# Gate product in single-pass operands, and a new VectorE order of states, sums and low parts around the plane copies

## Chip, cores and metric

The kernel runs on one core of one Trainium2 chip. The metric is the device time of one execution in microseconds (us). Before the change three runs gave 1149.07, 1149.14 and 1149.42 us; the median is 1149.14 us.

## What is computed

A two-layer encoder trunk over 512 tokens of width 1024. Layer 0 mixes tokens with two groups of gated linear attention heads, layer 1 with multi-head latent attention; each is followed by a squared-ReLU MLP. The change lies in layer 0's mixer, which in the reference is, per head:

```python
S_t = diag(exp(log_g_t)) S_{t-1} + k_t v_t^T ;  o_t = S_t^T q_t
# group A (HGRN2): forget = lb + (1-lb)*sigmoid(hf); k = 1-forget; log_g = log(forget)
# group B (GLA):   log_g = log_sigmoid(ga @ w_gate + b_gate) / 16
o = rmsnorm(o, norm) * silu(gate)
mix = concat([o_a, o_b]) @ w_out
```

`ga` has 16 columns and comes out of the input projection; `ga @ w_gate` is the gate product. The outputs are held to float32-like accuracy, so most products are made of three: an operand is split into a high part (an fp32r tile) and a low part (what is left), and high x low, low x high and high x high are summed (`mm3`, lines 1938 to 1940).

## The kernel before

The mixer's eight heads lie in six packs: two of GLA with two heads each, four of HGRN2 with one. The eight heads are numbered `o` = 0 to 7 in the order of the packs. A hand-written table, `SLOTS`, sets the order of the work on every engine: 46 slots, in each of which TensorE projects one tile (a key, query, value, gate or forget tile; 24 products of 128x512 for the projected ones) or turns a value tile or makes a gate product (`z`, slots 2 and 9). With each slot go, at fixed places, `items` (the decayed keys and queries of the pack ahead), `groups` (a step of the planes of the pack behind), `end` (the pack whose cumulative sums close the slot), and the lists OUTPUTS, SQUARES, SUMS and MIXES of heads.

The words of the trace's lines: a plane is one level of the masked key-query products of a head, made on TensorE in `pairs` (L2094, L2107) and copied through a mask by VectorE in `group` (L1539). A pack has seven planes, in the steps (0, 1), (2, 3), (4, 5), (6). After step 2 TensorE makes the chunk states (`chunk_states`, L2156) and VectorE chains them (`update_state`, L1513 and L1515). `outputs` (L2119, then L2123) waits for a head's plane 6 and, before L2123, for the pack's states. ScalarE squares the head's output (`head_square` L1039, `head_copy` L1045 and L1048), VectorE takes the square's low part (`square_low`, L1495), TensorE sums it (`head_sum`, L2134), ScalarE makes the inverse root (L898, L899), VectorE multiplies (`head_gate`, L1500 and L1503), ScalarE takes the high part (`head_high`, L1058) and VectorE the low part (`head_low`, L1507). `cumulate` (L1490) makes a pack's cumulative sums, from which GpSimd makes the differences `dec` (L831). `clamp` (L1457, L1462) reads a forget or gate tile out of its PSUM bank; ScalarE makes the sigmoid (L996 to L998); the gate's product with it is L1476. `split_high` (L636) and `split_low` (L645) split a weight unit.

Each engine runs its own list in order. Waits that matter here:

- One buffer, `sq[:, 1, :]`, holds the head being mixed. `head_copy` of head `o` (L1048) overwrites it and so waits until `head_low` of head `o - 1` has read it: `act.wait_ge(mix_ready, o)`. `head_sum(o)` waits for that copy: `pe.wait_ge(o_read, o + 1)`.
- Two PSUM banks take the projected tiles in turn. A bank is free when its tile two before has been read; for a gate tile that is when L1476 has run. Gate tile 7 is the last one (slot 37); after it TensorE fills the output projection's banks, token block 0 in the bank of gate 6, block 1 in the bank of gate 7.
- `pairs` of the last pack waits for the plane copies before it; `transpose_keys` waits for the states of the pack before.

In slot 21 (tile `q` of pack 3) VectorE's list is: `head_gate(0)`, three items, `cumulate(3)`, `head_low(0)`, `square_low(1)`, the step-2 `group` of heads 2 and 3 with the state, then slot 22. In slots 36 and 37 it is: items, `head_low(5)`, step-2 `group` of head 6 with the state, `clamp` of gate 7, the step-3 `group` of head 6.

Of the kernel before, what the change touches and what calls it, by code (L numbers as in the profile page):

```python
# [5 lines left out]
ALU = mybir.AluOpType  # L6
ACT = mybir.ActivationFunctionType
F32 = mybir.dt.float32
F32R = mybir.dt.float32r
# [3 lines left out]
P = 128  # L13
T = 512
# [7 lines left out]
HEADS = 4  # L22
GLA_DK = 64
GATE_RANK = 16
# [4 lines left out]
STEPS = [(0, 1), (2, 3), (4, 5), (6,)]  # L29
# [27 lines left out]
def trunk(nc, x, positions, norm_gains, ev_w_in, hg_lb_table, gla_w_gate, gla_b_gate, hg_out_norm,  # L57
# [39 lines left out]
    for st in range(8):  # L97
# [11 lines left out]
        n = len(long_)  # L109
# [3 lines left out]
        for a in range(1, n):  # L113
            i = long_[a]
# [43 lines left out]
    tile_no = {}  # L158
# [152 lines left out]
    with ExitStack() as ctx:  # L311
        def sb(name, shape, dt=F32, scope=ctx):
            return scope.enter_context(nc.sbuf_tensor(name, shape, dt))
# [15 lines left out]
        gbc = sb("gbc", [P, D])  # L329
        vec = sb("vec", [P, V_ROWS])  # L330
        lbt = sb("lbt", [P, 6, HEADS])
        w_gate = sb("w_gate", [2 * GATE_RANK, HEADS * GLA_DK])
        ropec = sb("ropec", [P, 2])
        tmp = sb("tmp", [P, 2, T])
        tok = sb("tok", [P, 16, NT])
# [13 lines left out]
        with ExitStack() as s1:  # L349
            sb("under_s1", [P, KD, 2, T], F32, s1)  # L350
            x_tok = sb("x_tok", [P, NT, D], F32, s1)
            vrows = sb("vrows", [V_ROWS, P], F32, s1)
        with ExitStack() as s2:
            sb("under_s2", [P, KD, 2, T], F32, s2)
            xl = sb("xl", [P, LEVELS, T], F32, s2)
            dec = sb("dec", [P, 3, T], F32, s2)
            kq_sb = sb("kq_sb", [P, 2, 2, T], F32, s2)
            b_sb = sb("b_sb", [P, T], F32, s2)
            qe0 = sb("qe", [P, T], F32, s2)
            vbuf = sb("vbuf", [P, 4, T], F32, s2)  # L360
            ke = sb("ke", [P, T], F32, s2)
            e_last = sb("e_last", [P, 2, NT], F32, s2)
            a_sb = sb("a_sb", [P, 4, P], F32, s2)
            ke_t = sb("ke_t", [P, NT - 1, P], F32, s2)
            state = sb("state", [P, NT - 1, P], F32, s2)
            t_f = sb("t_f", [P, T], F32, s2)
            t_g = sb("t_g", [P, T], F32, s2)
            ga_t = sb("ga_t", [2 * GATE_RANK, T], F32, s2)
        with ExitStack() as s3:
            sb("under_s3", [P, KD, 2, T], F32, s3)  # L370
            v_tok = sb("v_tok", [P, NT, D], F32, s3)
# [269 lines left out]
        def split_low(dve, u, i=0):  # L641
            dve.wait_ge(hi_ready, u + 1 + BODY * i)
            for src, hi, lo, g in pieces(u):
                if g is None:
                    ins = nc.vector.tensor_tensor(lo, src, hi.bitcast(F32), ALU.subtract)  # L645
                else:
                    ins = nc.vector.scalar_tensor_tensor(out=lo, in0=src, scalar=vec[:, g:g + 1], in1=hi.bitcast(F32),  # L647
                                                         op0=ALU.mult, op1=ALU.subtract)
            ins.then_inc(lo_ready, 1)
# [20 lines left out]
        def halves(ap, L):  # L670
            return ap.rearrange("p (b h j) -> p b h j", h=2, j=L)

        def gain(layer, n, k):
            c = gain_col(layer, n, k)
            return vec[:, c:c + 1]
# [121 lines left out]
        def _(pool):  # L797
# [4 lines left out]
            nc.gpsimd.affine_select(out=ident[:, :], in_=ident[:, :], compare_op=ALU.not_equal, fill=1.0, base=0,  # L802
                                    pattern=[[-1, P]], channel_multiplier=1).then_inc(consts_ready, 1)
            ch.link(nc.gpsimd.memset(masks[:, :, :], 0.0))
            for r, c in ((slice(0, 64), slice(64, 128)), (slice(0, 32), slice(32, 64)), (slice(64, 96), slice(96, 128))):
                ch.link(nc.gpsimd.memset(masks[r, 0, c], 1.0))
            for lv in range(2, LEVELS):
# [86 lines left out]
        def _(act):  # L894
# [73 lines left out]

            n = tile_no[("ga", 0)]
            wait_tile(act, n)  # L970
            nc.scalar.copy(ga_t[:, :], bank[n % 2][0:2 * GATE_RANK, :]).then_inc(ga_ready, 1)
            pump(unit_no[("ga", 0)])

            def decay(p, lv):
# [401 lines left out]
        def _(dve):  # L1376
# [41 lines left out]
            ch.link(nc.vector.tensor_tensor(lbt[:, 1, :], t0, lbt[:, 0, :], ALU.subtract))  # L1418
            nc.vector.tensor_tensor(lbt[:, 2, :], t1, lbt[:, 0, :], ALU.subtract).then_inc(vec_ready, 1)
            split_low(dve, 3)  # L1420
            dve.wait_ge(vec_ready, 3)
            ch.link(nc.vector.tensor_tensor(lbt[:, 0, :], lbt[:, 1, :], lbt[:, 2, :], ALU.add))
            ch.link(nc.vector.reciprocal(lbt[:, 3, :], lbt[:, 0, :]))
            ch.link(nc.vector.tensor_tensor(lbt[:, 4, :], lbt[:, 1, :], lbt[:, 3, :], ALU.mult))
            ch.link(nc.vector.tensor_scalar(lbt[:, 5, :], lbt[:, 4, :], -1.0, 1.0, ALU.mult, ALU.add))
            dve.wait_ge(x_split[START], 2 * NT)
            nc.vector.memset(pp[0][:, :, :], 0.0).then_inc(p_zero, 1)
            dve.wait_ge(consts_ready, 4)
# [93 lines left out]
            def group(lead, step):  # L1522
                heads = heads_of(PACK_OF[lead])
                if step == 0:
                    for o in heads:
                        if o < 4:
                            nc.vector.memset(a_bufs[o], 0.0).then_inc(a_zero, 1)
                        else:
                            dve.wait_ge(o_done, o - 3)
                for plane in STEPS[step]:  # L1530
                    for o in heads:
                        n = plane_no(o, plane)
                        dve.wait_ge(p_done, n + 1)
                        if plane:
                            dve.wait_ge(a_ready, plane_no(o, plane - 1) + 1)
                        elif o < 4:
                            dve.wait_ge(a_zero, o + 1)
                        mask = masks[:, plane:plane + 1, :].to_broadcast([P, NT, P])
                        nc.vector.copy_predicated(a_bufs[o % 4], mask.bitcast(I32), plane_bank(n)).then_inc(a_ready, 1)  # L1539
                if step == 2:  # L1540
                    update_state(PACK_OF[lead])

            for i, (tile, col, items, groups, end) in enumerate(SLOTS):
                if tile is not None:
                    if tile[0] in "fg":
                        clamp(*tile)
                    if i == IDLE_SLOT - 1:
                        for o, c in groups:
                            group(o, c)
                    if col is not None:  # L1550
                        wait_tile(dve, tile_no[tile])
                        if len(groups) < 2:
                            split_low(dve, unit_no[tile] + SPLIT - 1)
                    evacuate(*tile)
                if i == IDLE_SLOT:
                    split_low(dve, EO + SPLIT - 1)
                for o in SQUARES[i - 1] if i >= 1 else ():
                    if o not in WHOLE_SUMS + SOON_SUMS:
                        square_low(o)
                for o in MIXES[i]:  # L1560
                    head_gate(o)
                planes_first = len(items) > 4
                if planes_first:
                    for o, c in groups:
                        group(o, c)
                for p, lv in items:
                    decayed(p, lv)
                if end is not None:
                    cumulate(end)
                for o in MIXES[i]:  # L1570
                    head_low(o)
                for o in SQUARES[i]:
                    if o in SOON_SUMS:
                        square_low(o)
                for o, c in groups if not planes_first and i != IDLE_SLOT - 1 else ():
                    group(o, c)
                if col is not None and len(groups) > 1:
                    split_low(dve, unit_no[tile] + SPLIT - 1)
                if i in EXT_SLOTS:
                    split_low(dve, EXT_SLOTS[i])  # L1580
# [355 lines left out]
        def _(pe):  # L1936
# [111 lines left out]
            def project(tile, col):  # L2048
                n = tile_no[tile]
                what, i = tile  # L2050
                if what == "z":
                    pe.wait_ge(ga_ready, 1)
                    wait_bank(pe, n)
                    nc.tensor.matmul(bank[n % 2][:, :], w_gate[:, i * P:(i + 1) * P], ga_t[:, :], start=True,
                                     stop=True).then_inc(tile_done, 1)
                    return
                if what == "w":
                    pe.wait_ge(v_raw, i + 1)
                    if tile not in APART:
                        wait_bank(pe, n)  # L2060
                    elif i == 2:
                        pe.wait_ge(v_ready, 1)
                    for t in range(NT):
                        ins = nc.tensor.transpose(tile_bank(tile)[:, t * P:(t + 1) * P],
                                                  vbuf[:, i % 4, t * P:(t + 1) * P], ident[:, :])
                    ins.then_inc(tile_done, 1)
                    return
                feature_tile(unit_no[tile], n, h_hi, h_lo)
# [459 lines left out]
```

## Time and profile before

| | us |
|---|---|
| median of the three runs | 1149.14 |
| the profiled execution, its own time | 1148.82 |
| its span in the trace | 1147.10 |
| TensorE busy (98% of the span) | 1129.7 |
| VectorE busy (70%) | 802.0 |
| ScalarE busy (55%) | 626.9 |

All times below count from the span's start. The mixer of layer 0 takes about the first 250 us. A busy share of TensorE counts matmuls whose ends are modelled, so that the start-to-start step of matmuls (0.23 us for 128x512 in fp32r) says more than their durations (0.39 us). In a row of the timeline the bracket is the idle time of that engine ahead of the instruction, with what ended it.

### The profile page before, as it was taken

What the parts mean: (1) busy time and instruction counts of PE and PEld (TensorE: products, weight loads), DVE (VectorE), ACT (ScalarE), POOL (GpSimd) and SP (SyncE); (2) the same over time, 40 slices, a digit from 0 to 9 for tenths busy, and PEclk for the clock granted to TensorE, in tenths of its full rate; (3) what the DMA queues carried; (4) which work ended last, traced back from release to release, by engine and by line L of the source; (5) the groups of instructions that cost most, each with busy time, mean ns of one, the idle gap of its engine ahead of it and who ended that gap; (6) DMA issues with size and microseconds to landing.
All of it is one profiled execution on the core that took longest, in us unless ns stands there. A gap on an engine that the chain in (4) does not pass through costs nothing.

```text
span 1147.1 us, 18687 instructions
## 1 busy us (share of the span) xinstructions
PE 1129.7 (98%) x7053; PEld 941.4 (82%) x7053; DVE 802.0 (70%) x1197; ACT 626.9 (55%) x1168; POOL 130.4 (11%) x129
## 2 busy tenths in 40 slices
PE   9999999999999999999999999999999999999997
PEld 7787787778988888888888988888988888888886
DVE  6567888866578767767666578846578768768564
ACT  6654675646645554554447766646645545544432
POOL 2432333200222111110000001000000000000000
PEclk9999999999999999999999999999999999999999
DMA  5322222263233233231323323104342233231321
GB/s 173 102 81 57 76 56 57 75 202 110 90 123 110 92 110 128 74 127 37 110 81 82 107 56 91 47 27 139 110 147 93 88 114 110 91 111 42 105 74 74
DMA packets 87596, 108.36 MB, mean 94 GB/s; under 512 B 10290, under 2 KB 48291, under 8 KB 87524
## 3 DMA queue, kind: packets, MB, share of 16 engines
q1 hardware_dynamic: 85780, 101.87, 28.0%
q0 software_dynamic: 1744, 5.51, 1.6%
q8 instruction: 48, 0.79, 0.3%
q14 instruction: 24, 0.20, 0.1%
HBM read 104.22 MB, written 2.10 MB: 93 GB/s over the span
## 4 chain that ended last, share of the span: by engine, by line
PE 87%; DVE 6%; ACT 4%; issue 2%; DMA 0%; POOL 0%; DVEq 0%; ACTq 0%; SPq 0%
PE bank L1938 22%; PE bank L1940 22%; PE bank L1939 22%; PE pp L1938 3%; PE pp L1940 3%; PE pp L1939 3%; PE po L2466 2%; PE pp L2001 1%; PE po L1940 1%; PE po L1939 1%; PE po L1938 1%; PE pp L2447 1%; DVE tmp L1539 1%; ACT w_hi L638 1%; PE pp L2107 1%
## 5 line engine op out<-in xcount | busy, mean ns | idle before, releaser
L1938 PE MATMUL bank<-h_lo,w_hi 128*128 128x512 f32 (+1 forms) x724 | 277.2, 383 | 0.6 <-DVE y L1476 0.6
L1940 PE MATMUL bank<-h_hi,w_hi 128*128 128x512 f32 (+1 forms) x724 | 274.3, 379 | 0.0
L1939 PE MATMUL bank<-h_hi,w_lo 128*128 128x512 f32 (+1 forms) x724 | 274.3, 379 | 0.0
L1938 PEld LDWEIGHTS bank<-h_lo,w_hi 128*128 128x128 f32 x724 | 136.2, 188 | 28.4 <-issue 2.7
L1940 PEld LDWEIGHTS bank<-h_hi,w_hi 128*128 128x128 f32 x724 | 136.2, 188 | 25.7
L1939 PEld LDWEIGHTS bank<-h_hi,w_lo 128*128 128x128 f32 x724 | 136.2, 188 | 24.5
L636 ACT CAST wx<-raw 128x1024 fp32r<-128x1024 f32 x72 | 74.6, 1049 | 97.3 <-DVE raw L1631 66.0
L1938 PE MATMUL bank<-wx,a_hl 128*128 128x512 f32 x320 | 125.3, 392 | 0.0
L1940 PE MATMUL bank<-wx,a_hl 128*128 128x512 f32 x320 | 124.6, 389 | 0.0
L1939 PE MATMUL bank<-wx,a_hl 128*128 128x512 f32 x320 | 124.5, 389 | 0.0
L1642 DVE TENSOR_TENSOR y<-y,bank 128x512 f32<-128x512 f32 x80 | 54.8, 685 | 86.8 <-PE bank L1940 86.6
L645 DVE TENSOR_TENSOR wx<-raw,wx 128x1024 fp32r<-128x1024 f32 x72 | 87.9, 1221 | 28.2 <-ACT wx L636 27.9
L647 DVE SCALAR_TENSOR_TENSOR w_lo<-stage,vec,w_hi 128x512 fp32r<-128x512 f32 (+3 forms) x124 | 76.9, 672 | 9.8 <-ACT w_hi L638 9.8
L831 POOL TENSOR_TENSOR dec<-b_sb 128x512 f32<-128x512 f32 x48 | 67.2, 1422 | 142.6 <-DVE b_sb L1490 59.8
L638 ACT ACTIVATE w_hi<-stage,vec 128x512 fp32r<-128x512 f32 (+3 forms) x124 | 74.6, 656 | 14.9 <-DMA stage<-in_mlp_w 14.3
L645 DVE TENSOR_TENSOR w_lo<-stage,w_hi 128x1024 fp32r<-128x1024 f32 x44 | 57.5, 1308 | 21.0 <-ACT w_hi L636 11.7
L1940 PEld LDWEIGHTS bank<-wx,a_hl 128*128 128x128 f32 x320 | 60.1, 188 | 12.5
L1939 PEld LDWEIGHTS bank<-wx,a_hl 128*128 128x128 f32 x320 | 60.1, 188 | 12.2
L1938 PEld LDWEIGHTS bank<-wx,a_hl 128*128 128x128 f32 x320 | 60.1, 188 | 12.3
L636 ACT CAST w_hi<-stage 128x1024 fp32r<-128x1024 f32 (+1 forms) x45 | 46.1, 1026 | 14.5 <-DMA stage<-in_mlp_w 8.9
L1136 ACT ACTIVATE tmp<-bank 128x512 f32<-128x512 f32 x26 | 15.6, 598 | 59.9 <-PE bank L1940 59.7
L1938 PE MATMUL bank<-w_lo,a_hl 128*128 128x512 f32 x112 | 45.2, 404 | 0.0
(406 smaller groups left out, 2175.3 us busy)
## 6 DMA issues: line engine op xcount, KB each, us to landing
stage<-in_mlp_w SPq DMA_DIRECT2D x66, 512.0 KB, 3.8
raw<-in_mlp_w SPq DMA_DIRECT2D x50, 512.0 KB, 3.5
stage<-in_ev_w_in SPq DMA_DIRECT2D x28, 512.0 KB, 3.8
spare<-in_mlp_w SPq DMA_DIRECT2D x12, 512.0 KB, 4.6
stage<-in_ev_w_out SPq DMA_DIRECT2D x8, 512.0 KB, 3.5
stage<-in_od_w_out SPq DMA_DIRECT2D x8, 512.0 KB, 3.5
x_tok<-in_x SPq DMA_DIRECT2D x4, 512.0 KB, 4.9
xr<-in_x POOLq DMA_DIRECT2D x4, 512.0 KB, 4.3
```

The costliest lines, as they stand in the source:

```text
L636: ins = nc.scalar.copy(hi, src)
L638: ins = nc.scalar.activation(hi, src, ACT.Copy, scale=vec[:, g:g + 1])
L645: ins = nc.vector.tensor_tensor(lo, src, hi.bitcast(F32), ALU.subtract)
L647: ins = nc.vector.scalar_tensor_tensor(out=lo, in0=src, scalar=vec[:, g:g + 1], in1=hi.bitcast(F32), op0=ALU.mult, op1=ALU.subtract)
L831: nc.gpsimd.tensor_tensor(dec[:, item % 3, :].rearrange("p (b j) -> p b j", j=2 * L), b_sb[:, :].rearrange("p (b j) -> p b j", j=2 * L), r ...
L1136: nc.scalar.activation(f, src[:, :], ACT.Relu).then_inc(up_read, 1)
L1539: nc.vector.copy_predicated(a_bufs[o % 4], mask.bitcast(I32), plane_bank(n)).then_inc(a_ready, 1)
L1642: nc.vector.tensor_tensor(dst, dst, banks[src][:, :], ALU.add).then_inc(prod_read, 1)
L1938: nc.tensor.matmul(dst, wh, xl_, start=first, stop=False)
L1939: nc.tensor.matmul(dst, wl, xh, start=False, stop=False)
L1940: return nc.tensor.matmul(dst, wh, xh, start=False, stop=last)
L2466: ins = nc.tensor.matmul(po[:, kb * P:T], v_tok[:, kb, h * P:(h + 1) * P], turned_probs(h)[:, kb, kb * P:T], start=(kb == 0), stop=(kb == ...
```

## The change

1. The gate product. `ga_t` and the gate weights become fp32r tiles of 128 rows: rows 0 to 31 hold the high part, 32 to 63 the low part of `ga` against the high part of the weights, 64 to 95 the high part of `ga` against the low part of the weights, 96 to 127 zeros. One product over 128 rows gives the sum of all three.
2. `update_state` runs after the last step of a pack (plane 6) in place of after step 2.
3. In a slot with cumulative sums, and in slot 36, `cumulate` and `head_low` come behind the slot's plane copies. Of the slots with `head_low` that is slots 21 and 36. `cumulate` changes its place in slots 16, 21 and 27.
4. In slot 37 the `clamp` of gate 7 comes behind the slot's `group` (now with the state).

```diff
-        w_gate = sb("w_gate", [2 * GATE_RANK, HEADS * GLA_DK])
+        gate_w = sb("gate_w", [P, HEADS * GLA_DK], F32R)
...
-            ga_t = sb("ga_t", [2 * GATE_RANK, T], F32, s2)
+            ga_t = sb("ga_t", [P, T], F32R, s2)
...
+            ch.link(nc.gpsimd.memset(ga_t[6 * GATE_RANK:P, :].bitcast(F32), 0.0))
+            ch.link(nc.gpsimd.memset(gate_w[6 * GATE_RANK:P, :].bitcast(F32), 0.0))
...
-            nc.scalar.copy(ga_t[:, :], bank[n % 2][0:2 * GATE_RANK, :]).then_inc(ga_ready, 1)
+            nc.scalar.copy(ga_t[GATE_HIGH, :], bank[n % 2][0:2 * GATE_RANK, :]).then_inc(vec_ready, 1)
+            act.wait_ge(vec_ready, 4)
+            nc.scalar.copy(ga_t[GATE_HIGH_AGAIN, :], ga_t[GATE_HIGH, :].bitcast(F32)).then_inc(vec_ready, 1)
+            act.wait_ge(vec_in, 16 * 10)
+            for r in (GATE_HIGH, GATE_LOW):
+                nc.scalar.copy(gate_w[r, :], w_gate[:, :]).then_inc(vec_ready, 1)
...
+            dve.wait_ge(vec_ready, 4)
+            nc.vector.tensor_tensor(ga_t[GATE_LOW, :], bank[tile_no[("ga", 0)] % 2][0:2 * GATE_RANK, :],
+                                    ga_t[GATE_HIGH, :].bitcast(F32), ALU.subtract).then_inc(ga_ready, 1)
             dve.wait_ge(vec_ready, 3)
...
+            dve.wait_ge(vec_ready, 7)
+            nc.vector.tensor_tensor(gate_w[GATE_HIGH_AGAIN, :], w_gate[:, :], gate_w[GATE_HIGH, :].bitcast(F32),
+                                    ALU.subtract).then_inc(ga_ready, 1)
...
-                if step == 2:
+                if step == len(STEPS) - 1:
                     update_state(PACK_OF[lead])
...
-                    if tile[0] in "fg":
-                        clamp(*tile)
                     if i == IDLE_SLOT - 1:
                         for o, c in groups:
                             group(o, c)
+                    if tile[0] in "fg":
+                        clamp(*tile)
...
-                if end is not None:
-                    cumulate(end)
-                for o in MIXES[i]:
+                lows_first = i != IDLE_SLOT - 2 and end is None
+                for o in MIXES[i] if lows_first else ():
                     head_low(o)
                 for o in SQUARES[i]:
                     if o in SOON_SUMS:
                         square_low(o)
                 for o, c in groups if not planes_first and i != IDLE_SLOT - 1 else ():
                     group(o, c)
+                if end is not None:
+                    cumulate(end)
+                for o in MIXES[i] if not lows_first else ():
+                    head_low(o)
...
-                    pe.wait_ge(ga_ready, 1)
+                    pe.wait_ge(ga_ready, 2)
+                    pe.wait_ge(consts_ready, 4)
...
-                    nc.tensor.matmul(bank[n % 2][:, :], w_gate[:, i * P:(i + 1) * P], ga_t[:, :], start=True,
+                    nc.tensor.matmul(bank[n % 2][:, :], gate_w[:, i * P:(i + 1) * P], ga_t[:, :], start=True,
```

`SOON_SUMS` holds head 1 alone; its `square_low` is in slot 21. `IDLE_SLOT` is 38.

## Rows read from the trace of the kernel before

**Rows 1.** The page, part 1: busy time, share of the span, instructions of each engine.

```profile
PE 1129.7 (98%) x7053; PEld 941.4 (82%) x7053; DVE 802.0 (70%) x1197; ACT 626.9 (55%) x1168; POOL 130.4 (11%) x129
```

**Rows 2.** Waits of PE over the whole run: total us, times, longest.

```profile
PE po L2119 <- DVE tmp L1539: 3.9, 2, 2.4
```

**Rows 3.** Timeline, PE, the first gate product: start, us, engine, line, operation, tiles.

```profile
28.71 0.39 PE L1940 MATMUL bank<-h_hi,w_hi 128*128 128x512 f32 x1
29.03 1.12 PE L2054 MATMUL bank<-ga_t,w_gate 32*128 32x512 f32 x2
30.08 0.50 PE L1938 MATMUL bank<-h_lo,w_hi 128*128 128x512 f32 x1
```

**Rows 4.** Timelines of DVE, ACT and PE around the start of slot 0.

```profile
22.58 0.15 DVE L1422 TENSOR_TENSOR lbt<-lbt 128x4 f32<-128x4 f32 x1
...
25.77 1.23 DVE L645 TENSOR_TENSOR w_lo<-stage,w_hi 128x1024 fp32r<-128x1024 f32 x1 [1.21 <-ACT w_hi L636]
...
24.59 1.05 ACT L636 CAST w_hi<-stage 128x1024 fp32r<-128x1024 f32 x1 [2.35 <-DMA stage<-in_ev_w_in]
...
23.47 0.40 PE L1938 MATMUL bank<-h_lo,w_hi 128*128 128x512 f32 x1
```

**Rows 5.** Timeline, DVE, from the cumulative sums of slot 21 to the state.

```profile
127.00 1.36 DVE L1490 TENSOR_TENSOR_SCAN b_sb<-ones,t_f 128x128 f32<-128x128 f32 x4
128.28 0.67 DVE L1507 TENSOR_TENSOR a_hl<-sq,a_hl 128x512 fp32r<-128x512 f32 x1
128.86 0.69 DVE L1495 TENSOR_TENSOR sq_lo<-sq,sq_hi 128x512 fp32r<-128x512 f32 x1
129.46 0.74 DVE L1539 COPY_PREDICATED tmp<-gbc,pp 128x512 f32<-128x512 int32 x1
...
131.93 0.29 DVE L1513 COPY state<-misc 128x128 f32<-128x128 f32 x1
```

**Rows 6.** Timeline, ACT and PE, slots 21 and 22: copy and sum of head 1.

```profile
128.98 0.60 ACT L1048 ACTIVATE sq<-po 128x512 f32<-128x512 f32 x1 [2.70 <-DVE a_hl L1507]
...
129.77 0.42 PE L2134 MATMUL po<-sq_lo,ones 128*128 128x512 f32 x1
...
130.86 0.76 PE L2107 MATMUL pp<-kq_sb 64*32 64x32 f32 x64 [0.43 <-DVE rinv L1539]
```

**Rows 7.** Timeline, PE, slot 33: outputs of head 5 and the products behind.

```profile
199.65 1.13 PE L2119 MATMUL po<-tmp,vbuf 128*128 128x128 f32 x8 [1.54 <-DVE tmp L1539]
...
201.71 1.01 PE L2094 MATMUL pp<-xl 128*64 128x64 f32 x21
```

**Rows 8.** Timeline, DVE, slots 36 to 38.

```profile
226.28 0.68 DVE L1507 TENSOR_TENSOR a_hl<-sq,a_hl 128x512 fp32r<-128x512 f32 x1
226.88 1.58 DVE L1539 COPY_PREDICATED tmp<-gbc,pp 128x512 f32<-128x512 int32 x2
228.34 0.29 DVE L1513 COPY state<-misc 128x128 f32<-128x128 f32 x1
228.67 0.73 DVE L1515 SCALAR_TENSOR_TENSOR state<-state,e_last,misc 128x128 f32<-128x128 f32 x2
...
229.92 0.72 DVE L1539 COPY_PREDICATED tmp<-gbc,pp 128x512 f32<-128x512 int32 x1
...
232.09 0.69 DVE L1476 TENSOR_TENSOR y<-bank,t_g 128x512 f32<-128x512 f32 x1 [0.34 <-ACT t_g L998]
...
235.66 0.66 DVE L1495 TENSOR_TENSOR sq_lo<-sq,sq_hi 128x512 fp32r<-128x512 f32 x1
```

**Rows 9.** Timeline, PE, outputs of head 6, the fill of block 1, the sum.

```profile
230.79 1.95 PE L2119 MATMUL po<-tmp,vbuf 128*128 128x128 f32 x8 [2.40 <-DVE tmp L1539]
...
234.31 0.48 PE L1938 MATMUL bank<-w_lo,a_hl 128*128 128x512 f32 x1
...
237.93 0.50 PE L2134 MATMUL po<-sq_lo,ones 128*128 128x512 f32 x1
```

**Rows 10.** Windows: PE, PEld, DVE, ACT, POOL busy, PEclk, DMA share, GB/s.

```profile
232.00:233.00 1.00, 1.00 (x7) 1.00 (x7) 0.69 (x1) 0.99 (x2) 0.00 (x0) 0.50 0.29 25
```

More of the change, by code:

```diff
@@ L352, in trunk @@
             vrows = sb("vrows", [V_ROWS, P], F32, s1)
+            w_gate = sb("w_gate", [2 * GATE_RANK, HEADS * GLA_DK], F32, s1)
         with ExitStack() as s2:
@@ L671, in halves @@
             return ap.rearrange("p (b h j) -> p b h j", h=2, j=L)
+        GATE_HIGH, GATE_LOW, GATE_HIGH_AGAIN = [slice(r, r + 2 * GATE_RANK) for r in (0, 2 * GATE_RANK, 4 * GATE_RANK)]
         def gain(layer, n, k):
```

## The prediction, made before any run of the change

> **What bounds the kernel.** I read the page's busy shares first: TensorE is busy for 1129.7 of the span's 1147.10 us [rows 1], so time is won either by giving it less work or by closing its gaps. The list of its waits says where the gaps are that another engine makes: the largest entry is 3.9 us in two waits of `outputs` for a plane copy [rows 2]. The timelines put them at slot 33 (1.54 us, head 5) [rows 7] and behind slot 37 (2.40 us, head 6) [rows 9]. The second costs more than its 2.40 us: the granted clock, 1.0 before, reads 0.50 behind it (1.2 in place of 2.4 GHz) [rows 10]. From the outputs to the next product TensorE takes 234.31 - 230.79 = 3.52 us there [rows 9], and 201.71 - 199.65 = 2.06 us for the same work at slot 33 [rows 7], where the clock held. My price of one fall of the clock is the difference, about 1.5 us. Elsewhere TensorE runs without a gap and hands its delay on, so what slot 22 loses reaches the end.
>
> **Part 1, the gate product.** Two products stand on TensorE's path. For one, the start before it to the start behind it is 30.08 - 28.71 = 1.37 us [rows 3]. A 128x512 product in fp32r has a step of 0.23 us, so the same stretch would be 0.46 us and each product gives back 0.91 us: **-1.82 us** for two (the other, in slot 9, shows the same stretch). What bounds it: nothing, if the new product should run as the old one, and 2 x 0.91. I take the upper end, since an fp32r product over 128 rows is the kernel's commonest row [rows 3]. The row shows two records of the old product, in 1.12 us [rows 3]. The Trainium skill, "FP8 and Floating Point Precision", TensorE Precision Notes, says that a true FP32 product takes four passes through the array; by that rule three of four steps go, an estimate of 3 x 0.23 = 0.69 us for each product and a term of -1.38 us. The trace's stretch is longer than four steps, and the row decides.
>
> The operands cost work at the start, where I find cover for all. ScalarE adds one small copy and two casts; it stands idle 2.35 us for a load just there [rows 4], and three pieces of 32 rows cost no more than the 0.5 to 0.6 us that 512 columns cost it elsewhere [rows 6]. VectorE adds two low parts, 0.7 us each at most (0.69 us for 128x512 out of PSUM [rows 8]), ahead of an idle time of 1.21 us [rows 4]. The first of them now frees the bank that the `q` tile of slot 1 writes from 23.47 on [rows 4]: starting near 22.6, where L1422 stands now [rows 4], it ends near 23.3 and TensorE sees it near 23.4. The margin is 0.1 us; if it fails, it costs up to 0.5 us. GpSimd adds two memsets ahead of the masks' last flag, which nobody needs before about 24 us; no queue of loads is touched.
>
> **Part 2, slot 21.** This is the part that I think costs. Before, VectorE runs the sums at 127.00, `head_low(0)` at 128.28, `square_low(1)` at 128.86, four plane copies from 129.46 to 131.93 [rows 5]. After: `square_low` at 127.00, copies from 127.60 to 130.07 (2.47 us), sums to 131.35 (1.28 us), and `head_low(0)` only then, 131.35 in place of 128.28: 3.07 us later. ScalarE is standing in its list at the copy of head 1, L1048, for just that instruction: it waited 2.70 us and began 0.70 us behind the start of `head_low` [rows 6]. So the copy begins at 132.05, ends at 132.65, and `head_sum(1)` can start at 132.75. Before, it started at 129.77 with no idle ahead of it [rows 6]: TensorE now waits 2.98 us. The earlier copies spare it the 0.43 us that it waited for a plane at 130.86 [rows 6], and from 132.75 to the next planes is 0.55 us: they start at 133.30 in place of 130.86, **+2.44 us**. Queued behind the waiting copy on ScalarE are the value tile of slot 22, the inverse root and a weight's cast, all late by 3 us but none needed at once. On TensorE everything is queued behind it.
>
> Its idle time, less the modelled end of the last matmul, is about 2.8 us. One of 1.54 us left the clock alone, one of 2.40 us brought it down; 2.8 is nearest to the second, so I add one fall, **+1.5 us**, with 0 as the other end.
>
> In slots 16 and 27 `cumulate` moves too. There VectorE waits for TensorE's next tile afterwards, and GpSimd's differences are needed only in the items two slots on: nothing.
>
> **Part 3, states last.** In slot 33 the wait for head 5's plane ends earlier by the state's time, 228.34 to about 229.32 = 0.98 us by the same row elsewhere [rows 8]. I book no gain: from there to slot 37 VectorE's chain does not wait for TensorE, so TensorE arrives early and waits again. In the other packs no plane copy is waited for.
>
> **Part 4, slots 36 and 37.** Plane 6 of head 6 moves from 229.92 to 228.34 (copies from 226.28, then the low part of 0.60 us) [rows 8], 1.58 us earlier, and so `outputs(6)`, to 229.21, with a gap of 1.5 us ahead. But the clamp of gate 7 now stands behind that plane and the state and begins near 229.93 in place of 229.32. ScalarE's sigmoid and the product L1476 follow: 232.70 in place of 232.09 [rows 8]. That product frees the bank of block 1's fill. TensorE, through with outputs and transposes at about 231.3 at full clock, waits there about 2.15 us, to 233.48, against 234.31 before [rows 9]. The fill is 12 products of 0.23 us; `head_sum(6)` then meets the low part of its square, 0.61 us late, 236.27 in place of 235.66 [rows 8], done near 237.04. Before it ran at 237.93 [rows 9]: **-0.9 us**. The bounds are -1.58 us (the whole plane's gain) and +0.61 us (VectorE's delay passed on). A fall of the clock here would cost 1.5 us of this; 2.15 us lies between the two gaps known, in two pieces with 2 us of work between, so I take none.
>
> **Sum.** -1.82 + 2.44 + 1.5 - 0.9 = +1.2 us. On the profiled execution's own 1148.82 us (span 1147.10 and 1.72 around it) that is 1150.0; the median of the runs stands 0.32 us higher, so **1150.4 us**. What this measurement can tell from no change is about 0.2%, 2.3 us.
>
> **The rivals.**
> - *No fall of the clock* at slot 22: -1.82 + 2.44 - 0.9 = -0.3, 1148.9 us. For it: 2.8 us is beyond any gap seen here, so the fall is an inference from one row; against it, a shorter gap fell.
> - *Two falls*, the other side: the wait for gate 7's bank, which the later clamp makes, brings the clock down a second time. Place: ahead of block 1's fill; price: another 1.5 us, 1151.9 us in all, slower by 0.24%. It decides once 2.15 us is idle enough. For it: 2.15 is nearer to 2.40 than to 1.54. Against it: the 2 us of matmuls just before.
> - *No stall in slot 22*: if ScalarE's copy of head 1 comes in time after all, the term and its fall go, with 0.43 us: -1.82 - 0.43 - 0.9 = -3.15, 1146.0 us. Against it: ScalarE's 2.70 us wait for exactly this low part [rows 6], and a sum that started on time by 0.2 us only.
> - *The gate product is not shorter*, if it should still be made in passes: the first term goes, 1152.2 us. Against it: every split product's row.
>
> **How the numbers follow.** One fall (at either place; they cost the same) 0.40, none 0.20, two 0.22, no stall 0.10, no shorter product 0.03, something unseen 0.05, shared out. The likeliest is one fall, 1150.4 us. The range takes in none and two falls, 1148.9 to 1151.9, wider by up to 1 us below (the tail's better bound) and 0.6 us above (the start's margin): 1147.9 to 1152.5. Faster by over 0.2% (below 1146.8) needs the stall not to come: 0.12 with the unseen. Slower by over 0.2% (above 1151.4) is most of two falls, the longer product and the rest: 0.23. Within 0.2%: 0.65.
>
> **What would show it.** Part 1: L2054 with one record and a step of 0.23 us, twice, and slot 1's `q` tile starting without idle. Part 2: L2134 in slot 22 with about 3 us idle ahead of it, released by ScalarE's L1048, that by L1507 behind the scans, and PEclk 0.50 for some us behind. Part 3: no 1.54 us ahead of head 5's outputs, but the same time of head 6's to VectorE. Part 4: outputs of head 6 about 1.6 us earlier against VectorE, and a new wait of about 2 us ahead of block 1's fill, released by L1476. The prediction is wrong if `head_sum(1)` starts on time, if the clock stays at 1.0 throughout or falls twice, or if a gap behind 250 us swallows or adds some of it.

## The result, and the profile after

Seven runs of the changed kernel gave a median of **1152.86 us** (1152.26 to 1153.85), against 1149.32 for seven runs of the kernel before beside them. The ratio of the two is 1.0037, with a 95% interval from 1.0027 to 1.0046: slower by 3.5 us, or 0.3%. A later session gave 1152.56 against 1149.21, ratio 1.0031 [1.0020, 1.0042]. The forecast was 1150.4, and its range ended at 1152.5. The profiled execution took 1152.5 us. Of the fifteen runs of the two sessions the five slowest (1153.05 us and above) have a mean granted clock of 0.996 over the whole span, the ten others 0.997 or 0.998, as has the profiled one.

The page of the changed kernel, its span and part 1:

```profile
span 1150.8 us, 18690 instructions
...
PE 1129.0 (98%) x7051; PEld 941.4 (82%) x7051; DVE 802.7 (70%) x1199; ACT 628.6 (55%) x1171; POOL 133.5 (12%) x131
```

TensorE lost two of its records (the old gate products were two each) and is busy for about as long as before [rows 1]. The span grew by 3.7 us all the same, so the time went into gaps. The waits of PE, total us, times and longest, show which:

```profile
PE bank L1957 <- DVE y L1492: 3.6, 2, 2.1
PE po L2154 <- ACT sq L1058: 2.8, 1, 2.8
...
PE po L2139 <- DVE tmp L1555: 1.7, 2, 0.9
PE bank L1957 <- ACT kq_sb L1022: 1.1, 2, 0.6
```

The 3.9 us of `outputs` [rows 2] fell to 1.7. In their place stand 2.8 us of a head's sum (slot 22), a wait of 2.1 us at the fill for gate 7's product (its other entry, 1.5 us, is at slot 33), and, in the last row, two waits for `kq_sb` that the prediction does not contain. Their place is behind the two gate products. The timeline, PE and ACT:

```profile
29.52 0.40 PE L1959 MATMUL bank<-h_hi,w_hi 128*128 128x512 f32 x1
29.76 0.39 PE L2074 MATMUL bank<-ga_t,gate_w 128*128 128x512 f32 x1
30.70 0.47 PE L1957 MATMUL bank<-h_lo,w_hi 128*128 128x512 f32 x1 [0.55 <-ACT kq_sb L1022]
...
29.96 0.60 ACT L1022 ACTIVATE kq_sb<-bank 128x512 f32<-128x512 f32 x1 [1.76 <-PE bank L1959]
...
54.44 0.47 PE L1957 MATMUL bank<-h_lo,w_hi 128*128 128x512 f32 x1 [0.55 <-ACT kq_sb L1022]
```

The new product is one record of 0.39 us, as forecast. But the value tile behind it goes into the bank of the `q` tile two before it, and ScalarE can read that tile out (0.60 us) only after its last product of 29.52. From that product to the value tile is 1.18 us, against 1.37 before [rows 3]: 0.19 us won in place of 0.91. Of the whole old stretch, only this much stood beyond ScalarE's read.

Slots 21 and 22, timelines of DVE, ACT and PE:

```profile
127.41 0.69 DVE L1511 TENSOR_TENSOR sq_lo<-sq,sq_hi 128x512 fp32r<-128x512 f32 x1
128.01 0.74 DVE L1555 COPY_PREDICATED tmp<-gbc,pp 128x512 f32<-128x512 int32 x1
...
130.47 1.36 DVE L1506 TENSOR_TENSOR_SCAN b_sb<-ones,t_f 128x128 f32<-128x128 f32 x4
131.74 0.67 DVE L1523 TENSOR_TENSOR a_hl<-sq,a_hl 128x512 fp32r<-128x512 f32 x1
...
132.45 0.60 ACT L1058 ACTIVATE sq<-po 128x512 f32<-128x512 f32 x1 [5.75 <-DVE a_hl L1523]
...
133.19 0.47 PE L2154 MATMUL po<-sq_lo,ones 128*128 128x512 f32 x1 [2.84 <-ACT sq L1058]
...
133.92 0.90 PE L2127 MATMUL pp<-kq_sb 64*32 64x32 f32 x64
```

The low part stands behind the copies and the sums, 131.74 in place of 128.28 [rows 5]; the copy of head 1 follows 0.71 us behind its start, and the sum waits 2.84 us. The windows behind it (PEclk is the third column from the end) show what the gap brings:

```profile
133.00:134.00 1.00, 0.81 (x11) 0.38 (x19) 0.55 (x1) 0.53 (x2) 1.00 (x1) 0.82 0.00 0
134.00:135.00 1.00, 1.00 (x65) 0.94 (x66) 0.11 (x1) 0.94 (x2) 1.00 (x2) 0.50 0.23 55
...
136.00:137.00 1.00, 1.00 (x3) 0.75 (x3) 0.93 (x4) 0.32 (x1) 0.51 (x1) 0.50 0.90 269
137.00:138.00 1.00, 1.00 (x6) 0.78 (x5) 0.20 (x1) 0.00 (x0) 0.00 (x0) 0.97 0.03 8
```

The clock granted to TensorE is 1.2 GHz for a little over 3 us. Slots 33 and 37, timelines of PE and DVE:

```profile
203.18 1.13 PE L2139 MATMUL po<-tmp,vbuf 128*128 128x128 f32 x8 [0.80 <-DVE tmp L1555]
...
208.63 0.47 PE L1957 MATMUL bank<-h_lo,w_hi 128*128 128x512 f32 x1 [1.48 <-DVE y L1492]
...
233.68 1.13 PE L2139 MATMUL po<-tmp,vbuf 128*128 128x128 f32 x8 [0.89 <-DVE tmp L1555]
237.90 0.50 PE L1957 MATMUL bank<-w_lo,a_hl 128*128 128x512 f32 x1 [2.09 <-DVE y L1492]
...
241.54 0.50 PE L2154 MATMUL po<-sq_lo,ones 128*128 128x512 f32 x1
...
232.81 0.72 DVE L1555 COPY_PREDICATED tmp<-gbc,pp 128x512 f32<-128x512 int32 x1
...
234.39 0.68 DVE L1478 TENSOR_SCALAR t_g<-bank 128x512 f32<-128x512 f32 x1
...
237.15 0.69 DVE L1492 TENSOR_TENSOR y<-bank,t_g 128x512 f32<-128x512 f32 x1 [0.95 <-ACT t_g L1008]
```

At slot 33 the wait for the plane fell from 1.54 [rows 7] to 0.80, and TensorE waited longer at the next gate tile instead, 1.48 us against 0.61 before. At slot 37 the outputs waited 0.89 us in place of 2.40 [rows 9], and a new wait of 2.09 us stands ahead of the fill. In this execution the clock held there.

The lateness of the changed kernel against the trace of before, at six places, gives the balance (us; each term is the change of the lateness):

| from the row before to the row after | lateness | term | forecast |
|---|---|---|---|
| last product ahead of the first gate product, 28.71 to 29.52 | 0.81 | start +0.81 | 0 |
| value tile behind the second, 54.03 to 54.44 | 0.41 | gate products -0.40 | -1.82 |
| planes of slot 22, 130.86 to 133.92 | 3.06 | slot 22 +2.65 | +2.44 |
| clamp of the forget tile behind them, 137.32 to 141.59 | 4.27 | its half clock +1.21 | +1.5 |
| sum of head 6, 237.93 to 241.54 | 3.61 | tail -0.66 | -0.9 |
| span, 1147.1 to 1150.8 | 3.70 | rest +0.09 | 0 |

The rows of the half clock's term, DVE, before and after:

```profile
137.32 0.69 DVE L1457 TENSOR_SCALAR t_f<-bank 128x512 f32<-128x512 f32 x1 [1.93 <-PE bank L1940]
141.59 0.69 DVE L1473 TENSOR_SCALAR t_f<-bank 128x512 f32<-128x512 f32 x1 [4.39 <-PE bank L1959]
```

### The profile page after: what moved, and what is told of

It is laid out like the page before. It is cut to its first block, busy times and chain, and to the rows that moved or that the text cites. A ratio compares the mean times of both kernels' runs of the same rounds, so it can differ in the third digit from the quotient of the medians.

```text
span 1150.8 us, 18690 instructions
## 1 busy us (share of the span) xinstructions
PE 1129.0 (98%) x7051; PEld 941.4 (82%) x7051; DVE 802.7 (70%) x1199; ACT 628.6 (55%) x1171; POOL 133.5 (12%) x131
## 4 chain that ended last, share of the span: by engine, by line
PE 80%; DVE 4%; ACT 3%; issue 1%; DMA 0%; POOL 0%; DVEq 0%; ACTq 0%; SPq 0%
PE bank L1957 21%; PE bank L1959 20%; PE bank L1958 20%; PE pp L1957 3%; PE pp L1958 3%; PE pp L1959 3%; PE po L2486 2%; PE pp L2020 1%; PE po L1959 1%; PE po L1957 1%; PE po L1958 1%; PE pp L2467 1%; ACT w_hi L639 1%; DVE tmp L1555 1%; PE pp L2271 1%
## 5 line engine op out<-in xcount | busy, mean ns | idle before, releaser
L836 POOL TENSOR_TENSOR dec<-b_sb 128x512 f32<-128x512 f32 x48 | 69.6, 1471 | 143.8 <-DVE b_sb L1506 66.6
L646 DVE TENSOR_TENSOR w_lo<-stage,w_hi 128x1024 fp32r<-128x1024 f32 x44 | 56.7, 1289 | 19.9 <-ACT w_hi L637 10.8
```

What stands on the lines that cost most here:

```text
L836: nc.gpsimd.tensor_tensor(dec[:, item % 3, :].rearrange("p (b j) -> p b j", j=2 * L), b_sb[:, :].rearrange("p (b j) -> p b j", j=2 * L), r ...
```

## The experiments

Each ran beside the kernel before in its own session: that kernel's median was 1148.91 us for the first four, 1148.78 for the next four and 1149.21 for the last.

**Low part early (e1).** The change with one condition less, so that in slot 21 `head_low(0)` stands ahead of the copies again and the sums stay behind them:

```diff
-                lows_first = i != IDLE_SLOT - 2 and end is None
+                lows_first = i != IDLE_SLOT - 2
```

> The changed kernel, with one condition taken back: head_low stays ahead of the plane copies in the slots with cumulative sums (in effect slot 21). Theory A (the loss is head 1's sum in slot 22, which waits for ScalarE's copy, that for head_low(0) behind the sums, 2.8 us of idle time and about 1.4 us of a lowered clock): the wait ahead of head_sum(1) goes, the clock stays at 1.0 there, the 0.43 us wait for a plane goes too, and the time is 3.9 to 4.3 us below the changed kernel, about 1148.7. Rival B (the loss is the sums themselves, made later, so that GpSimd's differences come late): the sums still stand behind the planes, the time stays near 1152.9.

Measured: 1147.76 us, ratio 0.9996 [0.9987, 1.0005]. By the ratios that is 4.7 us less than the change, somewhat more than expected. The timeline, PE:

```profile
129.98 0.39 PE L2154 MATMUL po<-sq_lo,ones 128*128 128x512 f32 x1
...
130.53 0.76 PE L2127 MATMUL pp<-kq_sb 64*32 64x32 f32 x64
...
233.13 0.50 PE L1957 MATMUL bank<-w_lo,a_hl 128*128 128x512 f32 x1 [2.09 <-DVE y L1492]
```

Neither the sum nor the planes behind it wait. The place of one instruction in VectorE's list is the whole loss of slot 22.

**The gate product alone (e2).** The kernel before with part 1 of the change and VectorE's old order.

> The kernel before with the gate product's part of the change alone. As predicted before the result, it would be 1.8 us faster (1147.5). Theory A now: each shorter product only uncovers TensorE's wait for the bank that the q tile filled, until ScalarE has read it (about 0.55 us idle behind each product), so that 0.2 us each are left: -0.4 us, 1148.9. Rival C (the operands' work at the start delays the first projected tiles by the 0.7 us that the profile of the changed kernel shows): +0.3 us, 1149.6, with the q tile of slot 1 starting after an idle time that ends with VectorE's low part.

Measured: 1148.55 us, ratio 0.9994 [0.9985, 1.0003]: no change that can be told, and not the 1.82 us. Its trace has the two waits of 0.55 us for `kq_sb`, the first of them in this row of PE:

```profile
30.97 0.47 PE L1954 MATMUL bank<-h_lo,w_hi 128*128 128x512 f32 x1 [0.55 <-ACT kq_sb L1022]
```

**Sums and low part behind the planes alone (e3).** The kernel before with part 3 of the change in the slots with sums.

> The kernel before with one part alone: in the slots with cumulative sums, sums and head_low stand behind the plane copies. Theory A: this alone costs what the change costs in slot 22, 2.4 us of moved start and about 1.4 us of clock: +3.9 us, 1153.2, with the wait of 2.8 us ahead of head_sum(1) and PEclk 0.50 behind it. If the loss needs another part of the change as well: between 1149.3 and 1151.

Measured: 1153.45 us, ratio 1.0035 [1.0021, 1.0048]: alone, this part costs as much as the whole change. Its wait is longer than the 2.84 us, since the state still stands in slot 21 ahead of the sums. The timeline, PE:

```profile
134.10 0.77 PE L2137 MATMUL po<-sq_lo,ones 128*128 128x512 f32 x1 [3.63 <-ACT sq L1048]
```

**The tail alone (e4).** The kernel before with the states last and the new order in slots 36 and 37.

> The kernel before with the states last and the new order of slots 36 and 37 (low part behind the planes, clamp of gate 7 behind both groups). Theory A: outputs of head 6 come 1.6 us earlier, the fill of token block 1 waits some 2 us for gate 7's bank, the clock does not fall: -0.6 to -0.9 us, 1148.6. Rival D (a second fall of the clock at that wait): +0.7 us, 1150.

Measured: 1149.72 us, ratio 1.0005 [0.9996, 1.0014]. Timeline, PE:

```profile
229.30 1.13 PE L2122 MATMUL po<-tmp,vbuf 128*128 128x128 f32 x8 [0.76 <-DVE tmp L1539]
233.51 0.50 PE L1941 MATMUL bank<-w_lo,a_hl 128*128 128x512 f32 x1 [2.09 <-DVE y L1476]
```

Both waits are those of the changed kernel, but here the granted clock fell behind the second: 0.66, 0.50, 0.50 and 0.63 in the four us from 234 on.

**States last alone (e5).**

```diff
-                if step == 2:
+                if step == len(STEPS) - 1:
```

> The kernel before with the states updated last in each slot, and nothing else. In slot 37 the copy of plane 6 of head 6 no longer stands behind the state: it should begin at about 228.95 in place of 229.92, so head 6's outputs should start near 229.8 in place of 230.79, with about 1.4 us idle ahead. The clamp of gate 7 keeps its place, so its product with the sums, L1476, should stay at 232.09 and the fill of block 1 be released near 232.5 with a new wait of about 1 us. Theory A (the tail is a race of two chains, plane 6 and gate 7's product, and its price is the later of them plus a fall of the clock if a gap is long): both gaps are below 1.54 us, which left the clock alone, head 6's sum starts near 236.0 in place of 237.93, and the time is about 2 us below before. Rival B (what the tail gains is taken up by a later wait, as in slot 33): the same rows but a time within 0.5 us of before. Rival C (states last helps nothing, as the prediction booked for the other packs): head 6's outputs near 230.8 as before.

Measured: 1147.52 us, ratio 0.9989 [0.9980, 0.9998]. Timeline, PE:

```profile
230.44 1.13 PE L2119 MATMUL po<-tmp,vbuf 128*128 128x128 f32 x8 [1.56 <-DVE tmp L1539]
233.02 0.50 PE L1938 MATMUL bank<-w_lo,a_hl 128*128 128x512 f32 x1 [0.46 <-DVE y L1476]
```

This one line is worth 1.3 us, because plane 6 of head 6 then stands ahead of the state while gate 7's clamp keeps its early place. Both waits are short and the clock holds: theory A, with a smaller sum (about 2 us were expected). Against e4, the later clamp and low part of slots 36 and 37 give back 1.8 us (0.9989 to 1.0005), a fall of the clock included.

**A bank of their own for the gate products (e6, e9).** The test of the failed step: e6 is e2, and e9 the changed kernel, with the gate products in a PSUM bank outside the turn of the two. The tiles between the two gate products change banks with each other, so that the turn of the rest stays unbroken (not shown here):

```diff
-        APART = {("w", 0): po[:, :], ("w", 1): flat[3], ("w", 2): po[:, :]}
+        APART = {("w", 0): po[:, :], ("w", 1): flat[3], ("w", 2): po[:, :], ("z", 0): misc[:, :], ("z", 1): misc[:, :]}
...
-                    wait_bank(pe, n)
-                    nc.tensor.matmul(bank[n % 2][:, :], gate_w[:, i * P:(i + 1) * P], ga_t[:, :], start=True,
+                    if i >= 1:
+                        pe.wait_ge(z_read, i)
+                    nc.tensor.matmul(tile_bank(tile), gate_w[:, i * P:(i + 1) * P], ga_t[:, :], start=True,
```

> The kernel before with the new gate product alone, as in e2_gate_only, but the two gate products are written to a bank of their own, outside the turn of the two banks that the other tiles share. Theory A (the product is short, and what ate its gain is the wait of the next value tile for ScalarE's reading of the q tile, two tiles back in the same bank): the two waits of 0.55 us for kq_sb go, the stretch from the product before a gate product to the product behind it falls from 1.18 us in the changed kernel to about 0.5, and the time is about 1.3 us below e2_gate_only and 1.7 below before. Rival B (the value tile would wait for something else that ends at the same time, such as a transposed block or a weight): the waits stay at 0.5 us under another name and the time is that of e2_gate_only. Rival C (TensorE runs ahead by the 1.3 us and gives it back at the next wait of VectorE, at slots 33 and 37): the waits go but the time moves by less than 0.5 us.

Measured for e6: 1147.23 us, ratio 0.9980 [0.9971, 0.9989]. The timeline, PE, the product before, the gate product and the value tile, and then head 6's outputs:

```profile
29.69 0.40 PE L1960 MATMUL bank<-h_hi,w_hi 128*128 128x512 f32 x1
29.92 0.39 PE L2076 MATMUL misc<-ga_t,gate_w 128*128 128x512 f32 x1
30.16 0.39 PE L1958 MATMUL bank<-h_lo,w_hi 128*128 128x512 f32 x1
...
229.74 1.27 PE L2141 MATMUL po<-tmp,vbuf 128*128 128x128 f32 x8 [2.44 <-DVE tmp L1559]
```

The stretch is 0.47 us and the waits are gone: 0.90 us won for each product, the prediction's 0.91. By the ratios e6 is 1.6 us below e2, where 1.3 were expected.

> The changed kernel with its two gate products in a bank of their own, and nothing else different: the term that the prediction booked at 1.82 us and that came out near 0.4. The stretches around the gate products should fall from 1.18 us to 0.47 us as in e6_gate_own_bank. If what is won there reaches the end: about 1.4 us below the changed kernel of the same session. If slot 22's wait for VectorE takes it up (TensorE arrives 1.4 us earlier at the first heads' sum, and VectorE's chain does not follow TensorE there): the wait of 2.84 us grows by up to 1.4 us and the time is within 0.5 us of the changed kernel.

Measured for e9: 1151.10 us beside 1152.56 of the changed kernel in the same session, 1.46 us less (1150.09 to 1152.44 and 1151.61 to 1153.49); expected were 1.4. Its wait in slot 22 stayed at 2.84 us, so nothing was taken up there.

**Low part early and own bank (e7).** e1 and e9 together.

> The changed kernel with the sums behind the planes but the head's low part ahead of them in every slot (e1_low_early), and the gate products in a bank of their own. If the two terms add: e1_low_early showed 1147.8 us, so about 1.3 us less, 1146.5, without a wait at the first heads' sum and without the 0.55 us waits. If the gain of the gate products is taken up at VectorE's waits in slots 33 and 37 (TensorE arrives earlier and waits longer): the time is that of e1_low_early, and the waits ahead of outputs at slots 33 and 37 are longer by what was gained, which may also bring a fall of the clock at the second, +1.5 us.

Measured: 1146.81 us, ratio 0.9981 [0.9972, 0.9990], the first case. Some of the gain is lost where the clock falls behind the 2.09 us wait ahead of the fill, as it did in the profiled execution.

**Low part ahead of the sums (e10).** The changed kernel with these two exchanged:

```diff
-                if end is not None:
-                    cumulate(end)
                 for o in MIXES[i] if not lows_first else ():
                     head_low(o)
+                if end is not None:
+                    cumulate(end)
```

> The changed kernel with the head's low part still behind the plane copies in slot 21, but ahead of the sums, not behind them. The copy on ScalarE that waits for it should come 1.28 us earlier, and the wait of TensorE ahead of the first heads' sum be 2.84 - 1.28 = about 1.56 us, which is the length of the wait at slot 33 that left the clock alone. If the clock's fall hangs on the wait's length: no half clock behind it, and the time is 1.28 + 1.5 = 2.8 us below the changed kernel, near 1150.0. If any wait at this place brings the clock down: only 1.3 us below, near 1151.5.

Measured: 1151.16 us, 1.40 below the changed kernel's 1152.56. The number is that of the second case; the trace is not. Timeline and windows, PE:

```profile
131.92 0.47 PE L2154 MATMUL po<-sq_lo,ones 128*128 128x512 f32 x1 [1.58 <-ACT sq L1058]
```

```profile
133.00:134.00 1.00, 1.00 (x34) 0.87 (x26) 1.00 (x2) 0.97 (x3) 1.00 (x1) 1.00 0.00 0
236.00:237.00 1.00, 1.00 (x5) 0.77 (x4) 1.00 (x2) 1.00 (x4) 0.00 (x0) 0.64 0.34 129
237.00:238.00 1.00, 1.00 (x4) 0.81 (x3) 0.90 (x3) 1.00 (x2) 0.00 (x0) 0.50 0.30 59
```

The wait shrank to 1.58 us as worked out and the clock held behind it, but it fell at the tail, behind the same 2.09 us that had left it alone in the changed kernel. In this execution the fall was moved, not saved.

**Second looks (e11, e12).** The changed kernel and the kernel before, unaltered.

> The changed kernel unaltered, for the two runs above (same session) and for a second look at its start. In its first profile the first 16 transposes took 3.22 us against 2.60 before, and everything behind stood 0.73 us later. If that is chance of the execution: another duration between 2.5 and 3.6 us, as the ten profiles so far show for all kernels alike. If it belongs to the gate product's operands (two memsets of GpSimd more): again above 3.0 us.

> The kernel before unaltered, a second look at its start and at slot 37. If the start's length is chance: the first 16 transposes take another time than 2.60 us, up to 3.6 us. If the clock's fall behind slot 37 is chance too, as the two clusters of its times near 1148.2 and 1149.2 us suggest: a wait of about 2.4 us ahead of head 6's outputs with or without half clock behind it, and the time 1.0 us lower without.

Measured: 1152.56 us for the changed kernel, with the first 16 transposes in 3.06 us and the gate product at 29.50; one run of the kernel before at 1148.19 us, 1.0 us under that kernel's median of the session. The timeline, PE, first the row of its first profile, then two rows of this run, and a window of it:

```profile
7.90 2.60 PE L2001 MATMUL pp<-ident,xr 128*128 128x128 f32 x16
...
7.88 3.62 PE L2001 MATMUL pp<-ident,xr 128*128 128x128 f32 x16
...
231.61 1.13 PE L2119 MATMUL po<-tmp,vbuf 128*128 128x128 f32 x8 [2.36 <-DVE tmp L1539]
```

```profile
232.00:233.00 1.00, 1.00 (x11) 1.00 (x10) 0.66 (x2) 0.97 (x3) 0.00 (x0) 1.00 0.64 258
```

The start of the kernel before took 1 us longer here than in its first profile, without any gate operand, and longer than in both looks at the changed kernel. The weight loads of these transposes (count, shortest, median and longest in ns, first and last start in us), first profile and second look, show where the time lies:

```profile
L2001 PEld LDWEIGHTS pp<-ident,xr x16: 138/142/230, 7.7 to 10.1; 128*128 128x128 f32 x16
L2001 PEld LDWEIGHTS pp<-ident,xr x16: 230/230/230, 7.7 to 10.9; 128*128 128x128 f32 x16
```

The trace's record of the granted clock begins 9.0 us into the span in the first profile, 11.9 us here, and 10.8 and 10.3 us in the two of the changed kernel. Loads ahead of that moment take 230 ns, loads behind it about 140. So the start differs by execution, and the +0.81 in the balance is not shown to belong to the change. That a part of it does is not excluded: the transposes took 3.36 us on average in the nine profiles with the new operands and 2.94 in the five without, from 2.98 to 3.62 and from 2.52 to 3.62. And the clock held behind the 2.36 us that lie where it had fallen behind 2.40 [rows 9, 10].

**A version that beats both (e8).** The gate products in their own bank, each low part ahead of the planes, the sums behind them, the states last, and in slots 36 and 37 the order clamp of gate 7, planes of slot 36, plane 6, gate 7's product, low part.

> What the runs so far favour, together: the new gate product in its own bank, each head's low part ahead of the planes, the sums behind, states last, and in slots 36 and 37 an order that serves both chains: the clamp of gate 7 ahead of the planes of slot 36, and in slot 37 plane 6 first, then gate 7's product with the sums, then the low part. If the waits at the tail are what sets the time there, head 6's outputs start at about 1.5 us less against the changed kernel's chain and the fill of block 1 waits for less than 1 us, with no fall of the clock: gate products -1.7, slot 22's plane -0.4, the tail -2.2, some 4.3 us below before, near 1144.8 us. If the gains up to slot 33 are absorbed by VectorE's chain: -2.2 to -2.6 us, near 1146.5. If the clock falls at the tail nevertheless: 1.5 us more than either.

Measured: **1145.14 us** (1144.40 to 1145.28), ratio 0.9963 [0.9950, 0.9977], 3.6 us below before; some 4.3 were expected. The timeline, PE:

```profile
228.06 1.13 PE L2147 MATMUL po<-tmp,vbuf 128*128 128x128 f32 x8 [1.03 <-DVE tmp L1559]
229.95 0.48 PE L1964 MATMUL bank<-w_lo,a_hl 128*128 128x512 f32 x1
```

The fill runs straight behind the outputs, and the clock stays at 1.00 from where its record begins (12.4 us) through the rest of the mixer.

## Why the prediction came out too low

**Part 1, the step that failed.** "What bounds it: nothing, if the new product should run as the old one" was wrong: -0.40 us in place of -1.82. The price of the product was right, as e6 shows with 0.90 us each. What was missing is who else waits in that stretch. The trace of before has the row, in ScalarE's timeline:

```profile
29.14 0.60 ACT L1012 ACTIVATE kq_sb<-bank 128x512 f32<-128x512 f32 x1 [1.52 <-PE bank L1940]
```

The read of the `q` tile ends at 29.74, 0.34 us ahead of the value tile at 30.08 [rows 3]; the start after such a read costs TensorE another 0.14 us (29.96 + 0.60 to 30.70). That leaves 0.20 us to win, which is what came. The prediction asked what the operands cost and not which bank the next tile needs. Of its own signs for this part, the single record came; the step of 0.23 us did not, the start-to-start time behind the product is 0.94 us (29.76 to 30.70). The Trainium skill, "Perfetto Trace Analysis", Matmuls, asks that independent groups of matmuls rotate through PSUM banks, so that reading one out overlaps the next group; e6 and e9 agree: with two banks and a tile of one product the turn is too short, and a third bank brings 1.46 us. By the four passes of the Trainium skill, "FP8 and Floating Point Precision", TensorE Precision Notes, which the prediction weighed, each product would have given an estimated 0.69 us; e6 measures 0.90.

**The start.** Its margin held: from the transpose of `vrows` (18.70 before, 19.38 after) to the gate product (29.03 and 29.76) is 10.33 us before and 10.38 after. Of the 0.81 us by which the profile moved, 0.62 are the first transposes and 0.20 lie ahead of them (7.90 and 8.10); e11 and e12 show that such a start differs from one execution to the next.

**Part 2** was right. The sum was to start 2.98 us later; it started 3.42 later, less the 0.41 of lateness it came with, 3.01. The half clock cost 1.21 where 1.5 was taken. e1 and e3 show the cause from both sides. That the clock would fall was a step from one row on thin ground: in e12 it held behind 2.36 us at the very place of that row. Behind the 2.84 us and more of slot 22 it fell in all four profiles.

**Part 3** was right for slot 33: the gain was taken up at the next wait. **Part 4** gave -0.66 for -0.9, with the wait ahead of the fill at 2.09 us (2.15 forecast). The gap ahead of head 6's outputs was 0.89 us and not 1.5: what TensorE won at slot 33 it had given up at the gate tile there, so that it did not arrive early. The rival of two falls stayed out of both profiles of the changed kernel, and in part by luck: behind the same 2.09 us the clock fell in e4, e7 and e10. Whether a mean clock of 0.996 stands for a second fall or for a longer first one no trace shows; both profiles have 0.997.

With the gate products at -0.40 the prediction's own sum is 1150.4 + 1.42 = 1151.8 us, inside its range. The rest, up to 1152.86, is 1.0 us. The other terms of the balance, without the start, make 0.25 of it (+0.21 in slot 22, -0.29 for its clock, +0.24 at the tail, +0.09 behind), and the kernel before stood 0.18 higher beside these runs than the 1149.14 that the forecast started from. Some 0.6 us stay open. The start could hold some of it, which is not shown, and it is less than the spread between runs.

## What to carry to other kernels

When an operation on the bounding engine gets shorter, look up what the next one waits for besides: the read of a buffer two steps back, hidden until then, is the new bound, and its row in the old trace gives the margin. An instruction moved behind a group of others is late by that group for every engine that waits for it, so follow each of its readers to the engine that bounds. And where two chains meet at one place, as plane 6 and gate 7 do, an order that helps one by delaying the other wins little; interleave them.

## What the runs showed of the hardware

- **A wait of 2.1 to 2.4 us brings TensorE's clock down in some executions and not in others.** In twelve profiles with such a wait at the tail it fell to 1.2 GHz in six (2.09 us three times, and 2.26, 2.40, 2.44) and held in six (2.09 four times, 2.29, 2.36). Of the six that held, four had had a fall in slot 22, some 100 us earlier; of the eight without such a fall, two held. Behind 1.52 to 1.59 us it held (seven waits); behind 2.84, 2.85 and 3.63 us it fell (four waits). What decides between was not found.
- A fall lasted a little over 3 us in the changed kernel, but about 6.8 us of half clock stand behind the same 2.84 us wait in e9, and behind the 3.63 us in e3.
- **The start of one kernel differs by 1 us between executions.** The first 16 transposes took from 2.52 to 3.62 us over fourteen profiles. The trace's record of the granted clock begins between 9.0 and 12.4 us into the span, and the later it begins, the longer they take (within 0.1 us). A window ahead of the record prints 1.00 although nothing is recorded there; the durations of the weight loads, 230 ns ahead of that moment and about 140 behind it, tell more. The Trainium skill, "TensorE: Matmul & The Clock Gate", Part 1, says that the number of slow products at a kernel's start differs between runs of one kernel; the two looks at the kernel before agree, with six of the sixteen weight loads at 230 ns in one and all sixteen in the other.
